# PEER layer tail on one core: four of the dense blocks' eight slots go to the ring of gathered V rows, and tile 0's products lead tile 1's by two blocks

## The chip, the core and the metric

The kernel runs on one core of a Trainium2 chip. The metric is the time of one execution on the device in microseconds (us), lower is better. The version before takes 1754.23 us, the median of 3 runs (1752.3 to 1754.84).

## What is computed

The reference is one decoder layer over 256 tokens of width 2048: attention and short convolution, an output projection, a layer norm, and then the channel mixing that this change is about. For each token it picks 8 heads x 16 experts out of 16384, and each expert is one row of 2048 floats in `expert_u` and one in `expert_v`:

```python
eid = i1 * N_KEYS + i2                      # N_KEYS = 128, 16384 experts
g = softmax(best_s)
a = gelu(einsum('td,thkd->thk', hx, expert_u[eid]))
y = einsum('thk,thkd->td', g * a, expert_v[eid])
out = layernorm(ALPHA * h + y)
```

All arrays are float32. A row is 8 KB, and one pick (one row for each of 128 tokens) is 1 MB. There are 256 picks: 2 tiles of 128 tokens, 8 heads (a head of a tile is a unit, n = 0 to 15), 16 picks k each. In the kernel a pick has the number m = 16 n + k.

## The kernel before, in words

The engines run their own programs and wait for one another on semaphores. The order of each engine's work is written out by hand.

**U.** GpSimd gathers the 256 picks of `expert_u` by indirect DMA into a ring of RU = 8 slots (`gather_u`). VectorE takes the dot product of each with the tokens (`dot`, L1764), which counts `dots_done` and frees the slot.

**V, picks 0 to 143.** GpSimd also gathers the picks of `expert_v`, into a ring of RV = 7 slots (`gather_v`, L542 for units 0 to 13, L545 for units 14 and 15). TensorE adds the first PE_PICKS = 144 of them into PSUM with diagonal weights (L976), which counts `v_used`.

**V, picks 144 to 255.** VectorE adds these to `xh` (`add_row`, L1799), in the order of m, once its dots are all done. Each addition is followed by a drain that counts `v_dve`, and the gather of pick m waits for the addition of pick m - 7. This stage begins at 1409.9 us of the trace. Ahead of pick 246 VectorE waits for tile 0's four PSUM banks (`t0_sum`, L1851), ahead of pick 248 it waits for the two rows of layer norm 2 and finishes tile 0 (L1811, L1856, L1859), ahead of pick 253 it adds tile 1's banks (`t1_sum`, L1863), and behind pick 255 comes tile 1's layer norm (L1867 to L1874) with its output.

**Dense blocks.** The last FD = 40 of the 128 first keys, 5120 rows of `expert_v`, are not gathered for units 0 to 13: the gather has a bound (`bounds_check=ROWS - 1`), and a pick at or above it brings no row. These rows are read whole instead, as 40 blocks of 128 rows (1 MB each), by SyncE's DMA (L429). TensorE multiplies each block with a matrix of coefficients of tile 0 and one of tile 1: `dense_mm(t, f)` at L946 is four matmuls of 128x512. The matrices themselves are made by `hot_rows` (VectorE), `dense_rows` (TensorE, L938) and `dense_out` (ScalarE). The blocks lie in the eight slots of the U ring, free once U has ended: block f goes to slot f % 8. The first eight wait for the last dots, the others for tile 1's product:

```python
for f in range(FD):
    if f < RD:
        sp.wait_ge(S["dots_done"], TOPK * NU - RU + f + 1)
    else:
        sp.wait_ge(S["dense_used"], f - RD + 1)
```

and TensorE's order is

```python
for f in range(FD + LEAD):
    if f < FD:
        pe.wait_ge(s_d[f % RD], 16 * (f // RD + 1))
        dense_mm(0, f)
    if f >= LEAD:
        dense_mm(1, f - LEAD)
```

with LEAD = 3: the products of tile 0 run three blocks ahead of those of tile 1, and a slot is free when tile 1's product of its block has ended (`dense_used`). Behind block 39 SyncE issues the loads of the two rows of layer norm 2 (L431).

Of the kernel before, what the change touches and what calls it, by code (L numbers as in the profile page):

```python
# [7 lines left out]
ALU = mybir.AluOpType  # L8
# [21 lines left out]
TOPK = 16  # L30
NU = 16
RU = 8
RV = 7
# [2 lines left out]
PH = 8  # L36
V0_PICKS = TOPK * PH
PE_PICKS = V0_PICKS + TOPK
RD = 8
FD = 40  # L40
FA = 24
ROWS = (NKEY - FD) * NKEY
LEAD = 3
G_TOK = 8
NG_T = P // G_TOK
PICKS = (P, P - 2 * TOPK)
# [1 line left out]
IDS_AT.update({(n, 1): n + 1 for n in range(1, 9)})  # L48
HOT0_AT = {180 + 5 * b // 2: b for b in range(NG_T)}
HOT1_AT = {14 * TOPK + 5 + 3 * b // 2: b for b in range(NG_T)}  # L50
HTW = SEQ + 2
TCOL = (slice(0, P), slice(P + 2, SEQ + 2))
JOBS = [(0, (0,)), (1, (0,)), (0, (1,)), (1, (1,))] + [(h, (0, 1)) for h in range(2, PH)]
# [69 lines left out]
def build(nc, x, w_in, cmp_k_pos, cmp_k_w1, cmp_k_b1, cmp_k_w2, cmp_v_pos, cmp_v_w1, cmp_v_b1, cmp_v_w2,  # L123
# [15 lines left out]
    def at(name, shape, dt, offset=None):  # L139
        n = 2 if dt is BF16 else 4  # L140
        for s in shape[1:]:
            n *= s
        if offset is None:
            offset, top[0] = top[0], top[0] + (n + 31) // 32 * 32
        assert offset + n <= nc.sbuf_usable_end, name
        return nc.alloc_sbuf_tensor_at(name, shape, dt, offset=offset)
# [14 lines left out]
    xh = at("xh", [P, 2, D], F32, oc + 16 * K)  # L161
# [59 lines left out]

    hT = at("hT", [P, KC, HTW], F32, o_act)
    mixr = at("mixr", [P, KC, P], F32, o_act + 16 * K + 512)
# [35 lines left out]
    gate = at("gate", [P, NU, TOPK], F32, o_lo + 5 * K)  # L259
# [7 lines left out]
    eps2 = at("eps2", [P, 1], F32, o_lo + 6 * K + 448)  # L267
    qp = at("qp", [P, 2, 2, HTW], F32, o_lo + 6 * K + 512)
    stT = at("stT", [2, 2, P], F32, o_lo + 11 * K)
# [10 lines left out]
    v_home = [oc + 64 * K + 8 * K * i for i in range(4)] + [oc + 32 * K, oc + 40 * K, o_act]  # L280
    u_slot = [at(f"u_slot{i}", [P, D], F32, u_home[i]) for i in range(RU)]
    v_slot = [at(f"v_slot{i}", [P, D], F32, v_home[i]) for i in range(RV)]
    diag = at("diag", [P, 2, TOPK, P], F32, oc + 48 * K)
    sum0 = at("sum0", [P, D], F32, oc + 56 * K)
    ln2g_sb = at("ln2g_sb", [P, D], F32, oc + 48 * K)
# [29 lines left out]
    S = {n: nc.alloc_semaphore(n) for n in names}  # L315
# [5 lines left out]
    s_wb = [nc.alloc_semaphore(f"s_wb{i}") for i in range(4)]  # L321
    s_u = [nc.alloc_semaphore(f"s_u{i}") for i in range(RU)]
    s_v = [nc.alloc_semaphore(f"s_v{i}") for i in range(RV)]
    s_d = [nc.alloc_semaphore(f"s_d{i}") for i in range(RD)]

    def bview(i, *shape):
# [37 lines left out]
    def _(sp):  # L364
# [58 lines left out]
# [5 lines that stand above are left out]
            first = ROWS + NKEY * f  # L428
            sp.dma_start(u_slot[f % RD][:, :], expert_v[0][first:first + NKEY, :]).then_inc(s_d[f % RD], 16)  # L429
        for row, src in ((ln2g_sb, ln2_g), (ln2b_sb, ln2_b)):  # L430
# [11 lines left out]
    def _(pool):  # L442
# [86 lines left out]
        def gather_v(n, k):  # L529

            m = TOPK * n + k
            if m == 0:
                pool.wait_ge(S["wq_used"], 12)
            if m == EARLY_V:
                pool.wait_ge(S["wq_used"], 16)
            if RV <= m < PE_PICKS + RV:
                pool.wait_ge(S["v_used"], m - RV + 1)
            if m >= PE_PICKS + RV:
                pool.wait_ge(S["v_dve"], m - RV - PE_PICKS + 1)
            src = bass.IndirectOffsetOnAxis(ap=eid[:, n, k:k + 1], axis=0)  # L540
            if n < NU - 2:
                nc.gpsimd.indirect_dma_start(out=v_slot[m % RV][:, :], out_offset=None, in_=expert_v[0], in_offset=src,  # L542
                                             bounds_check=ROWS - 1, oob_is_err=False).then_inc(s_v[m % RV], 16)
            else:
                nc.gpsimd.indirect_dma_start(out=v_slot[m % RV][:, :], out_offset=None, in_=expert_v[0], in_offset=src  # L545
                                             ).then_inc(s_v[m % RV], 16)

        for m in range(TOPK * AHEAD):
            gather_u(m // TOPK, m % TOPK)
            if m == TOPK * AHEAD - 9:  # L550
                for k in range(EARLY_V):
                    gather_v(0, k)
        sent = TOPK * AHEAD
        for m in range(EARLY_V, TOPK * NU):
            while sent < min(TOPK * NU, TOPK * AHEAD + (m + 1) * 13 // 10):
                gather_u(sent // TOPK, sent % TOPK)
                sent += 1
            if m == PE_PICKS:
                while sent < TOPK * NU:
                    gather_u(sent // TOPK, sent % TOPK)  # L560
                    sent += 1
            gather_v(m // TOPK, m % TOPK)
# [3 lines left out]
    def _(pe):  # L566
# [375 lines left out]
        def dense_mm(t, f):  # L942

            src = dense0[:, f, :] if t == 0 else dense1[f >= FA][:, f - FA * (f >= FA), :]
            for q in range(4):
                ins = nc.tensor.matmul(bank[(4 if t == 0 else 0) + q][:, :], src, u_slot[f % RD][:, 512 * q:512 * q + 512],  # L946
                                       start=False, stop=(f == FD - 1))
                if f == FD - 1:
                    ins.then_inc(S[("t0_sum", "t1_sum")[t]], 1)
            if t and f < FD - RD:  # L950
                ins.then_inc(S["dense_used"], 1)
# [30 lines left out]
        for q in range(4):  # L982
            nc.tensor.matmul(bank[4 + q][:, :], ident[:, :], sum0[:, 512 * q:512 * q + 512], start=True, stop=False)
# [7 lines that stand above are left out]
# [381 lines left out]
    def _(dve):  # L1372
        V = nc.vector
# [404 lines left out]
        def hot_rows(t, b):  # L1778

            g, n = NG_T * t + b, PICKS[t]  # L1780
            cols = slice(G_TOK * b, G_TOK * b + G_TOK)
            if b == 0:
                dve.wait_ge(S["pick_ok"], t + 1)
            if g >= 2:
                dve.wait_ge(S["dense_mm"], g - 1)
            row, key, coef = (pickT[0:n, t, i, cols].unsqueeze(2) for i in range(3))
            V.tensor_tensor(hot1[0:n, g % 2, :, :], iota_row[0:n, :].unsqueeze(1).to_broadcast([n, G_TOK, FD]),
                            row.to_broadcast([n, G_TOK, FD]), ALU.is_equal)
            V.tensor_tensor(hot2[0:n, g % 2, :, :], iota_key[0:n, :].unsqueeze(1).to_broadcast([n, G_TOK, NKEY]),
                            key.to_broadcast([n, G_TOK, NKEY]), ALU.is_equal)  # L1790
            dve.drain()
            V.tensor_tensor(hot1[0:n, g % 2, :, :], hot1[0:n, g % 2, :, :], coef.to_broadcast([n, G_TOK, FD]), ALU.mult
                            ).then_inc(S["hot_ok"], 1)

        def add_row(m):

            n, k = divmod(m, TOPK)
            dve.wait_ge(s_v[m % RV], 16 * (m // RV + 1))
            V.scalar_tensor_tensor(xh[:, 1, :], v_slot[m % RV][:, :], gate[:, n, k:k + 1], xh[:, 1, :], ALU.mult, ALU.add)  # L1799
            dve.drain().then_inc(S["v_dve"], 1)  # L1800

        def stats_of(t):
# [16 lines left out]
        for n in range(NU):  # L1819
            for k in range(TOPK):  # L1820
# [15 lines left out]
                m = TOPK * n + k  # L1836
                if m in HOT0_AT:
                    hot_rows(0, HOT0_AT[m])
                if m in HOT1_AT:
                    hot_rows(1, HOT1_AT[m])  # L1840
        for b in range(len(HOT1_AT), NG_T):
            hot_rows(1, b)
        V.tensor_scalar(xh[:, 1, :], xh[:, 1, :], ALPHA, None, ALU.mult)
        dve.drain()
        for m in range(PE_PICKS, TOPK * NU):
            if m == PE_PICKS + TOPK:
                gates_of(NU - 1)
            if m == TOPK * NU - 10:
                for q in range(4):
                    dve.wait_ge(S["t0_sum"], q + 1)  # L1850
                    V.bn_stats(l2st[:, 0, q, :], bank[4 + q][:, :])  # L1851
                stats_of(0)
            if m == TOPK * NU - 8:
                dve.wait_ge(S["s_ln2row"], 32)
                root_inverse(0)
                V.scalar_tensor_tensor(y0[:, :], psum_all[:, 4:8, :].rearrange("p a b -> p (a b)"), l2mv[:, 0, 0:1],  # L1856
                                       ln2g_sb[:, :], ALU.subtract, ALU.mult)
                dve.drain()
                V.scalar_tensor_tensor(y0[:, :], y0[:, :], l2rs[:, 0:1], ln2b_sb[:, :], ALU.mult, ALU.add  # L1859
                                       ).then_inc(S["final_ok"], 1)  # L1860
            if m == TOPK * NU - 3:
                dve.wait_ge(S["t1_sum"], 4)
                V.tensor_tensor(xh[:, 1, :], xh[:, 1, :], psum_all[:, 0:4, :].rearrange("p a b -> p (a b)"), ALU.add)  # L1863
                dve.drain()
            add_row(m)
# [35 lines left out]
```

## Time and profile before

| | before |
|---|---|
| median of 3 runs | 1754.23 us (1752.3 to 1754.84) |
| the profiled execution, its own time | 1752.67 us |
| its span, first to last instruction | 1750.9 us |
| mean granted TensorE clock | 0.933 |
| VectorE busy | 1360.2 us (78%) |
| TensorE matmul busy | 1487.4 us (85%) |
| DMA, mean over the span | 351 GB/s |
| dense loads, issue to landing (median of 40) | 8.8 us |

All times of the trace are counted from the span's start. The 1752.67 us of the profiled execution are its span and 1.8 us around it. TensorE's matmul time is written by the profiler's model of pipelined instructions; a group of a float32 product shows 8 matmul instructions for the four of the program. "Idle before" is the time in which an engine had nothing running ahead of an instruction, with the one whose end let it go. A DMA's time to landing runs from its issue to its semaphore. PEclk is the granted TensorE clock in parts of full speed (2.4 GHz; the other level is half of it).

### The profile page before, as it was taken

How to read it: one execution, taken by the hardware profiler on the slowest of the kernel's cores; microseconds unless marked ns; L12 is line 12 of the kernel's file. 1: busy time of each engine (PE TensorE's matmuls, PEld its weight loads, DVE VectorE, ACT ScalarE, POOL GpSimd, SP SyncE). 2: the span in 40 equal slices, each digit the busy share in tenths (PEclk: the TensorE clock that was granted, in tenths of full speed). 3: DMA queues.
4: the chain of work that ended last, by engine and by line, in shares of the span. 5: the costliest groups of instructions: out<-in, count | busy, mean ns of one | idle time of the engine just before them, and what ended most of it. 6: DMA issues, size and time to landing. Idle time of an engine off the chain costs nothing.

```text
span 1750.9 us, 16867 instructions
## 1 busy us (share of the span) xinstructions
PE 1487.4 (85%) x6164; PEld 931.8 (53%) x6164; DVE 1360.2 (78%) x1915; ACT 380.5 (22%) x822; POOL 967.4 (55%) x591
## 2 busy tenths in 40 slices
PE   8999999999979906887777877888989899999940
PEld 7988999988668702333333333344445644444420
DVE  6666656666897999767868788977876988788798
ACT  5665455564201212101010101020220100000000
POOL 3210000000364677887777767786785887688581
PEclk9999999999989957989998999999999899999975
DMA  9876443466799999999999999999999999999994
GB/s 319 279 262 217 121 145 121 145 203 230 297 380 412 374 424 425 412 425 426 421 424 426 415 425 422 420 426 409 415 427 360 377 414 409 401 404 410 423 428 186
DMA packets 159379, 615.38 MB, mean 351 GB/s; under 512 B 20915, under 2 KB 74255, under 8 KB 96703
## 3 DMA queue, kind: packets, MB, share of 16 engines
q0 software_dynamic: 79232, 485.32, 67.6%
q1 hardware_dynamic: 80064, 128.99, 20.7%
q8 instruction: 48, 0.79, 0.2%
q14 instruction: 35, 0.29, 0.0%
HBM read 683.42 MB, written 2.10 MB: 392 GB/s over the span
## 4 chain that ended last, share of the span: by engine, by line
PE 29%; POOL 19%; DMA 19%; DVE 18%; issue 12%; DVEq 2%; ACT 1%; SPq 0%; POOLq 0%; ACTq 0%
DMA v_slot<-in_expert_v_dram,eid 15%; PE psum_all L587 13%; POOL v_slot L542 11%; DVE u_slot L1764 9%; POOL u_slot L525 9%; PE psum_all L727 4%; DVE xh L1799 4%; PE psum_all L976 3%; DMA u_slot<-in_expert_u_dram,eid 2%; PE psum_all L752 2%; PE psum_all L708 1%; PE psum_all L614 1%; PE psum_all L612 1%; PE psum_all L938 1%; DMA wq_ring<-in_w_query_dram 0%
## 5 line engine op out<-in xcount | busy, mean ns | idle before, releaser
L976 PE MATMUL psum_all<-v_slot,diag 128*128 128x512 f32 x1152 | 557.2, 636 | 154.5 <-DMA v_slot<-in_expert_v_dram,eid 108.9
L1764 DVE SCALAR_TENSOR_TENSOR u_slot<-u_slot,xh 128x2048 f32<-128x2048 f32 x256 | 576.2, 2287 | 91.3 <-DMA u_slot<-in_expert_u_dram,eid 90.0
L525 POOL DMA_INDIRECT u_slot<-in_expert_u_dram,eid x256 | 441.7, 1726 | 302.7 <-DVE u_slot L1764 136.7
L542 POOL DMA_INDIRECT v_slot<-in_expert_v_dram,eid x224 | 424.6, 1895 | 94.5 <-issue 64.7
L976 PEld LDWEIGHTS psum_all<-v_slot,diag 128*128 128x128 f32 x1152 | 224.1, 202 | 464.1 <-issue 255.4
L1799 DVE SCALAR_TENSOR_TENSOR xh<-v_slot,gate,xh 128x2048 f32<-128x2048 f32 x112 | 263.4, 2352 | 53.9 <-DMA v_slot<-in_expert_v_dram,eid 46.3
L1382 DVE TENSOR_TENSOR w_lo<-w_ring,w_hi 128x512 fp32r<-128x512 f32 x240 | 156.6, 688 | 78.3 <-ACT w_hi L1012 75.1
L587 PE MATMUL psum_all<-act_hi,w_hi 128*128 128x256 f32 x640 | 185.2, 289 | 1.1 <-DVE w_lo L1382 1.0
L587 PE MATMUL psum_all<-act_hi,w_lo 128*128 128x256 f32 x640 | 181.1, 283 | 0.0
L587 PE MATMUL psum_all<-act_lo,w_hi 128*128 128x256 f32 x640 | 181.0, 283 | 0.0
L1012 ACT ACTIVATE w_hi<-w_ring 128x512 fp32r<-128x512 f32 x240 | 139.4, 622 | 42.7 <-PE psum_all L587 41.5
L946 PE MATMUL psum_all<-u_slot,dense 128*128 128x512 f32 x320 | 143.4, 592 | 0.0
L752 PE MATMUL psum_all<-hT,wq_ring 128*128 128x258 f32 (+2 forms) x640 | 119.6, 346 | 11.9 <-DMA wq_ring<-in_w_query_dram 11.9
L587 PEld LDWEIGHTS psum_all<-act_hi,w_hi 128*128 128x128 f32 x640 | 122.4, 191 | 13.3 <-issue 4.1
L587 PEld LDWEIGHTS psum_all<-act_lo,w_hi 128*128 128x128 f32 x640 | 122.5, 191 | 2.8 <-issue 0.5
L587 PEld LDWEIGHTS psum_all<-act_hi,w_lo 128*128 128x128 f32 x640 | 122.5, 191 | 0.0
L752 PEld LDWEIGHTS psum_all<-hT,wq_ring 128*128 128x128 f32 x640 | 104.4, 194 | 27.9 <-DMA wq_ring<-in_w_query_dram 12.3
L513 POOL DMA_DIRECT2D skeys<-in_sub_keys_dram x1 | 1.2, 1165 | 198.1 <-PE psum_all L587 198.1
L946 PEld LDWEIGHTS psum_all<-u_slot,dense 128*128 128x128 f32 x320 | 60.8, 190 | 76.5 <-issue 76.5
L946 PE MATMUL psum_all<-u_slot,dense1a 128*128 128x512 f32 x192 | 86.3, 592 | 0.0
L545 POOL DMA_INDIRECT v_slot<-in_expert_v_dram,eid x32 | 64.2, 2005 | 34.2 <-DVEq L1800 26.6
L938 PEld LDWEIGHTS psum_all<-hot,hot 128*128 128x128 f32 (+1 forms) x512 | 65.2, 200 | 19.3 <-issue 13.6
(283 smaller groups left out, 1484.2 us busy)
## 6 DMA issues: line engine op xcount, KB each, us to landing
w_ring<-in_w_in_dram SPq DMA_DIRECT2D x88, 512.0 KB, 4.9
u_slot<-in_expert_v_dram SPq DMA_DIRECT2D x40, 1024.0 KB, 8.8
wo_ring<-in_w_out_dram SPq DMA_DIRECT2D x32, 512.0 KB, 5.0
wq_ring<-in_w_query_dram SPq DMA_DIRECT2D x32, 512.0 KB, 8.9
w_ring<-in_cmp_k_w_dram POOLq DMA_DIRECT2D x16, 512.0 KB, 5.7
w_ring<-in_cmp_v_w_dram POOLq DMA_DIRECT2D x16, 512.0 KB, 4.4
u_slot<-in_expert_u_dram,eid POOLq DMA_INDIRECT x256, 19.2
v_slot<-in_expert_v_dram,eid POOLq DMA_INDIRECT x256, 18.2
```

The lines of the kernel that those rows point to most:

```text
L525: nc.gpsimd.indirect_dma_start(out=u_slot[m % RU][:, :], out_offset=None, in_=expert_u[0], in_offset=bass.IndirectOffsetOnAxis(ap=eid[:, n ...
L542: nc.gpsimd.indirect_dma_start(out=v_slot[m % RV][:, :], out_offset=None, in_=expert_v[0], in_offset=src, bounds_check=ROWS - 1, oob_is_er ...
L587: ins = nc.tensor.matmul(o, st, mv, start=(k == 0 and b == 0 and i == 0), stop=(k == KC - 1 and i == 2), skip_group_check=True)
L727: ins = nc.tensor.matmul(bank[acc + b][:, :], st[:, k, half], mv[:, n % RING, :], start=(i == 0 and m == 0), stop=(i == KC - 1 and m == 2))
L752: ins = nc.tensor.matmul(bank[QBANK[h % 2] + c][:, cols], wq_ring[j % 2][:, k // 4, k % 4, 256 * (h % 2) + 128 * c:256 * (h % 2) + 128 * c ...
L938: ins = nc.tensor.matmul(bank[4 * t + g % 2][:, FD * i:FD * i + FD], hot2[0:n, g % 2, i, :], hot1[0:n, g % 2, i, :], start=True, stop=True ...
L946: ins = nc.tensor.matmul(bank[(4 if t == 0 else 0) + q][:, :], src, u_slot[f % RD][:, 512 * q:512 * q + 512], start=False, stop=(f == FD - 1))
L976: ins = nc.tensor.matmul(bank[(4 if n < PH else 0) + q][:, :], diag[:, n % 2, k, :], v_slot[m % RV][:, 512 * q:512 * q + 512], start=(m in ...
L1012: nc.scalar.activation(w_hi[:, n % RING, :], raw_item(n), ACT.Copy).then_inc(S["hi_done"], 1)
L1382: V.tensor_tensor(w_lo[:, n % RING, :], raw_item(n), w_hi[:, n % RING, :].bitcast(F32), ALU.subtract).then_inc(S["lo_done"], 1)
L1764: V.scalar_tensor_tensor(u_slot[m % RU][:, :], u_slot[m % RU][:, :], 1.0, xh[:, n // PH, :], ALU.mult, ALU.mult, accum_out=u_dot[:, n, k:k ...
L1799: V.scalar_tensor_tensor(xh[:, 1, :], v_slot[m % RV][:, :], gate[:, n, k:k + 1], xh[:, 1, :], ALU.mult, ALU.add)
```

## The change

`RD`, the number of slots for dense blocks, goes from 8 to 4: block f goes to U slot f % 4, and its load waits for tile 1's product of block f - 4. `LEAD` goes from 3 to 2. U slots 4 to 7 are appended to the V ring as its places 7 to 10. Picks up to 150 keep their places (m % 7). From m = 151 (`LATE`) on, the ring has 11 places, taken in the order of `RING_V`: first U slots 4 to 7, for picks 151 to 154, which wait for the dots 253 to 256; then the seven old places, whose gathers wait for the addition of pick m - 11. `v_place(m)` gives the place, `v_times(m)` how often it has been filled.

```diff
-RD = 8
+RD = 4
-LEAD = 3
+LEAD = 2
+LATE = V0_PICKS + TOPK + RV
+RING_V = list(range(RV, RV + RU - RD)) + [m % RV for m in range(V0_PICKS + TOPK, LATE)]
...
+def v_place(m):
+    return m % RV if m < LATE else RING_V[(m - LATE) % len(RING_V)]
+
+
+def v_times(m):
+    return sum(1 for i in range(m + 1) if v_place(i) == v_place(m))
...
     v_slot = [at(f"v_slot{i}", [P, D], F32, v_home[i]) for i in range(RV)]
+    v_slot += u_slot[RD:]
...
     s_v = [nc.alloc_semaphore(f"s_v{i}") for i in range(RV)]
+    s_v += [nc.alloc_semaphore(f"s_e{i}") for i in range(RU - RD)]
     s_d = [nc.alloc_semaphore(f"s_d{i}") for i in range(RD)]
...
-            if m >= PE_PICKS + RV:
-                pool.wait_ge(S["v_dve"], m - RV - PE_PICKS + 1)
+            if LATE <= m < LATE + RU - RD:
+                pool.wait_ge(S["dots_done"], TOPK * NU - RU + v_place(m) - RV + RD + 1)
+            if m >= LATE + RU - RD:
+                pool.wait_ge(S["v_dve"], m - len(RING_V) - PE_PICKS + 1)
```

The rest of the diff puts `v_place(m)` and `v_times(m)` where `m % RV` and `m // RV + 1` stood, in `gather_v` and in `add_row`.

## Rows read from the trace of the kernel before

**Rows 1.** The page: DMA busy in tenths, 40 slices

```profile
DMA  9876443466799999999999999999999999999994
```

**Rows 2.** Windows: PE, PEld, DVE, ACT, POOL busy (x), PEclk, DMA share, GB/s

```profile
1475.00:1500.00 25.00, 25.00 (x60) 11.08 (x59) 18.56 (x9) 0.00 (x0) 19.74 (x9) 1.00 1.00 402
1675.00:1700.00 25.00, 9.47 (x23) 3.86 (x21) 23.80 (x11) 0.00 (x0) 21.95 (x11) 0.76 1.01 428
```

**Rows 3.** Waits by engine from 1409 us on: total, times, longest

```profile
DVE xh L1799 <- DMA v_slot<-in_expert_v_dram,eid: 46.3, 49, 2.6
```

**Rows 4.** Timeline of VectorE: start, us, instructions, idle before them

```profile
1409.93 7.30 DVE L1799 SCALAR_TENSOR_TENSOR xh<-v_slot,gate,xh 128x2048 f32<-128x2048 f32 x3
1418.35 2.35 DVE L1799 SCALAR_TENSOR_TENSOR xh<-v_slot,gate,xh 128x2048 f32<-128x2048 f32 x1 [1.11 <-DMA v_slot<-in_expert_v_dram,eid]
...
1658.88 44.35 DVE L1799 SCALAR_TENSOR_TENSOR xh<-v_slot,gate,xh 128x2048 f32<-128x2048 f32 x18 [1.96 <-DMA v_slot<-in_expert_v_dram,eid]
1703.35 2.49 DVE L1851 BATCH_NORM_STATS2 l2st<-psum_all 128x6 f32<-128x512 f32 x4
...
1711.80 2.35 DVE L1856 SCALAR_TENSOR_TENSOR y<-psum_all,l2mv,ln2g_sb 128x2048 f32<-128x2048 f32 x1
...
1728.84 2.29 DVE L1863 TENSOR_TENSOR xh<-xh,psum_all 128x2048 f32<-128x2048 f32 x1
```

**Rows 5.** Timeline of TensorE: dense products, early and at the end

```profile
1423.37 3.60 PE L946 MATMUL psum_all<-u_slot,dense1a 128*128 128x512 f32 x8
1426.81 3.60 PE L946 MATMUL psum_all<-u_slot,dense 128*128 128x512 f32 x8
...
1667.14 3.60 PE L946 MATMUL psum_all<-u_slot,dense 128*128 128x512 f32 x8
1670.57 13.90 PE L946 MATMUL psum_all<-u_slot,dense1b 128*128 128x512 f32 x32
```

**Rows 6.** Timeline of SyncE: one dense load, and the last loads

```profile
1427.00 0.33 SPq L429 DMA_DIRECT2D u_slot<-in_expert_v_dram  x1
...
1639.87 0.33 SPq L429 DMA_DIRECT2D u_slot<-in_expert_v_dram  x1
```

**Rows 7.** Dense loads to landing: issued 1425-1622, 1622-1650, 1380-1400

```profile
DMA to landing us min/median/max: 8.2/8.7/9.5
DMA to landing us min/median/max: 9.0/9.4/9.5
DMA to landing us min/median/max: 10.0/11.1/12.2
```

**Rows 8.** Timeline of TensorE: a product that waited, and the next

```profile
1318.03 3.70 PE L976 MATMUL psum_all<-v_slot,diag 128*128 128x512 f32 x8 [0.89 <-DMA v_slot<-in_expert_v_dram,eid]
1321.57 1.88 PE L938 MATMUL psum_all<-hot,hot 96*128 96x40 f32 x16
```

**Rows 9.** Landing: gathers 1475-1500, 1600-1625; dense loads in these windows

```profile
DMA to landing us min/median/max: 17.3/19.0/19.8
DMA to landing us min/median/max: 12.8/13.9/15.2
DMA to landing us min/median/max: 8.4/8.6/8.8
DMA to landing us min/median/max: 8.3/8.4/8.6
```

**Rows 10.** Timeline of GpSimd: gathers 149 and 151

```profile
1400.47 10.25 POOL L542 DMA_INDIRECT v_slot<-in_expert_v_dram,eid  x1 [0.30 <-issue]
...
1413.46 2.17 POOL L542 DMA_INDIRECT v_slot<-in_expert_v_dram,eid  x1 [0.30 <-issue]
```

**Rows 11.** DMA issues: size, median us to landing

```profile
ln2b_sb<-in_ln_b_dram SPq DMA_DIRECT2D x1, 1024.0 KB, 17.9
```

**Rows 12.** Windows ahead of the dense stage, as rows 2

```profile
1200.00:1225.00 25.00, 23.06 (x86) 12.85 (x85) 16.62 (x18) 1.31 (x3) 15.60 (x10) 0.93 0.98 399
1225.00:1250.00 25.00, 23.74 (x86) 12.52 (x84) 22.68 (x24) 8.82 (x23) 18.60 (x11) 1.00 1.00 408
```

More of the change, by code:

```diff
@@ L537, in gather_v @@
                 pool.wait_ge(S["v_used"], m - RV + 1)
-            if m >= PE_PICKS + RV:
-                pool.wait_ge(S["v_dve"], m - RV - PE_PICKS + 1)
+            if LATE <= m < LATE + RU - RD:
+                pool.wait_ge(S["dots_done"], TOPK * NU - RU + v_place(m) - RV + RD + 1)
+            if m >= LATE + RU - RD:
+                pool.wait_ge(S["v_dve"], m - len(RING_V) - PE_PICKS + 1)
             src = bass.IndirectOffsetOnAxis(ap=eid[:, n, k:k + 1], axis=0)
             if n < NU - 2:
-                nc.gpsimd.indirect_dma_start(out=v_slot[m % RV][:, :], out_offset=None, in_=expert_v[0], in_offset=src,
-                                             bounds_check=ROWS - 1, oob_is_err=False).then_inc(s_v[m % RV], 16)
-            else:
-                nc.gpsimd.indirect_dma_start(out=v_slot[m % RV][:, :], out_offset=None, in_=expert_v[0], in_offset=src
-                                             ).then_inc(s_v[m % RV], 16)
+                nc.gpsimd.indirect_dma_start(out=v_slot[v_place(m)][:, :], out_offset=None, in_=expert_v[0], in_offset=src,
+                                             bounds_check=ROWS - 1, oob_is_err=False).then_inc(s_v[v_place(m)], 16)
+            else:
+                nc.gpsimd.indirect_dma_start(out=v_slot[v_place(m)][:, :], out_offset=None, in_=expert_v[0], in_offset=src
+                                             ).then_inc(s_v[v_place(m)], 16)
         for m in range(TOPK * AHEAD):
@@ L1797, in add_row @@
             n, k = divmod(m, TOPK)
-            dve.wait_ge(s_v[m % RV], 16 * (m // RV + 1))
-            V.scalar_tensor_tensor(xh[:, 1, :], v_slot[m % RV][:, :], gate[:, n, k:k + 1], xh[:, 1, :], ALU.mult, ALU.add)
+            dve.wait_ge(s_v[v_place(m)], 16 * v_times(m))
+            V.scalar_tensor_tensor(xh[:, 1, :], v_slot[v_place(m)][:, :], gate[:, n, k:k + 1], xh[:, 1, :], ALU.mult, ALU.add)
             dve.drain().then_inc(S["v_dve"], 1)
```

## The prediction

> **What bounds the kernel now.** I read the page first [rows 1]. No compute engine fills the span, but the 16 DMA engines stand at nine tenths or more from the twelfth slice to the last but one. So the tail, where the change works, is first of all a matter of who gets the DMA. The windows of 25 us [rows 2] say how the tail looks inside: in the dense stage TensorE is never idle (25.00 of 25 us) and the DMA share is 1.00 at 402 GB/s, while VectorE has gaps (18.56 us busy); once the dense blocks are in, the DMA moves 428 GB/s and VectorE has 23.80 us of its own work. The waits [rows 3] give these gaps a sum: 46.3 us in 49 waits for gathered V rows. VectorE's timeline [rows 4] gives them a place: they lie between 1418 and 1659 us. Once the dense loads are over (the last is issued at 1639.87 [rows 6]) the eighteen additions from 1658.88 run without a gap, 2.47 us each (44.35 for 18, with the drains between), and so does all that follows to the end. The end of the kernel is therefore VectorE's: from the first statistics of tile 0 at 1703.35 to the end of the span at 1750.9 there are 47.5 us of its work and of the output, with no wait worth a line.
>
> TensorE has no say in that end. Its timeline [rows 5] has one dense product of four matmuls every 3.433 us (1423.37 to 1426.81), a pair of them, tile 0's and tile 1's, every 6.87 us. Tile 0's last product starts at 1667.14 and ends at 1670.7, and the statistics that need it start at 1703.35: 32.6 us of slack. Tile 1's last product ends at 1684.5 and is needed at 1728.84 [rows 4]. The question is what the change does with this slack.
>
> **Part 1, the dense loads with four slots and a lead of two.** I call iteration j the pair that starts with tile 0's product of block j and goes on with tile 1's of block j - 2. The slot of block j - 4 is free at the end of iteration j - 2. Load j is issued then, and iteration j, the next but one, needs it. Between lies one iteration, 6.87 us. (Before, with eight slots and a lead of three, a slot was free at the end of iteration j - 5 and the load had four iterations, 27.5 us. That is why no wait is seen.)
>
> How long does a load take from slot to product? Three terms. From tile 1's product to the issue: the first such load goes at 1427.00 [rows 6], the next product starts at 1426.81 [rows 5], so 0.2 us. From issue to landing: 8.7 us in the median of 29 loads from 1425 to 1622, 8.2 at least, 9.5 at most, and 9.4 for the three behind 1622, when the gathers bring whole picks (units 14 and 15 have no bound) [rows 7]. From landing to the restarted product: a product that waited for its gather holds TensorE for 3.54 us until the next instruction in place of 3.43 (1318.03 to 1321.57 [rows 8]), 0.11 us, and I add 0.04 for the wake-up. Sum 0.2 + 8.7 + 0.15 = 9.05 us, against 6.87 that are covered. TensorE waits 2.18 us.
>
> Not at every block, though. If iteration j waits, iteration j + 1 does not: its load left at the end of iteration j - 1, and when iteration j starts late by 2.18, the next starts 6.87 later still, 2.18 + 6.87 = 9.05 behind that load's start. The recurrence is start(j) = the larger of start(j-1) + 6.87 and start(j-2) + 6.87 + 9.05, and it gives one wait in every two blocks: at 4, 6, ... 38, 18 waits. The gathers without a bound start at pick 224; in the changed kernel they are issued from about 1590 us on (80 additions from 1409.93 at 2.5 to 2.6 us, less the 11 of the ring), so I take the last 6 waits at 9.4 + 0.35 - 6.87 = 2.88 and the first 12 at 2.18. Sum 12 x 2.18 + 6 x 2.88 = 26.2 + 17.3 = 43.4 us.
>
> The smaller lead also moves tile 0's last product behind one more of tile 1's: without waits it would start at 1670.57 and end at 1674.2 [rows 5]. With them it ends at 1674.2 + 43.4 = 1717.6. The last of the four statistics (0.62 us each [rows 4]) ends 0.6 us later, at 1718.2. Before it ended at 1703.35 + 2.49 = 1705.8. **Difference +12.4 us.** Behind it follow the same additions and norms as before, 45.1 us to the end of the span. Tile 1's last product comes 10.3 us behind tile 0's (three more products) and is needed 23 us behind the statistics: hidden.
>
> Bounds: with every load at the shortest of the tail, 8.2, a wait is 1.68 and the sum 30.2, so tile 0's sum ends at 1704.4 and the statistics at 1705.0: -0.8 us. With every load at 9.5, 18 x 2.98 = 53.6: +22.6 us. The loads issued from 1380 to 1400 took 10.0 to 12.2 [rows 7], but they followed each other more closely than one load's time and lay behind one another in their queue; here the spacing is 6.87 or 9.05 us. At 10.0 the same sum gives +31.6, at 11.1 +51.4.
>
> Does the longer V ring slow the loads? The gathers' own times say how much stands in their queue: 19.0 us to landing from 1475 to 1500, 13.9 from 1600 to 1625. The dense loads of the same windows took 8.6 and 8.4 [rows 9]. So a queue of gathers that is a third deeper moves a dense load by 0.2 us, and I keep 8.7. The Trainium skill, "DMA: Bandwidth & Descriptors", section "Queues, rings and completion order", has it the same way: an engine takes turns between the queues it has work for, packet by packet, so the depth of the other queue would not matter. The section "Anatomy of one DMA" of the same page of the Trainium skill has some 2.0 us fixed and 436 GB/s (fitted to GpSimd's DMAs); with half the turns for a load of 1 MB, that is an estimate of 2.0 + 2 x 2.4 = 6.8 us, a wait of 0.3 us in place of 2.18, and no loss at all. The measured 8.7 us speaks against it, and the sum goes by the measurement.
>
> **Part 2, eleven places for V.** The gathers stay on GpSimd's one queue. Gather 149 stands from 1400.47 to 1410.7, 150 is next, and 151 starts at 1413.46 [rows 10]. All dots are over when the additions begin at 1409.93 [rows 4]. So the new, earlier permission of pick 151 (dot 253) brings nothing: the queue in front of it is what holds it. From 153 on the gathers no longer wait for an addition seven picks back. The bytes do not change (112 gathers, 40 blocks), nor does the DMA share of 1.00, so what VectorE wins of its 46.3 us is what the dense loads give up: with 43 us of waits the dense stream is about five blocks behind at 1650, which is five to seven picks for V, or some 12 us. VectorE would then reach pick 246 at about 1691 (in no case before 1703.35 - 46.3 = 1657) and stand there until tile 0's sum is done. The gain is real and is thrown away ahead of t0_sum. I cost it at zero; its cover is the wait for TensorE.
>
> **Part 3, what else moves.** Dense loads 4 to 7, issued behind the last dots before, now leave from 1423 on [rows 5]. That helps the first V rows (VectorE waits less around 1420), and again ends in the same wait: zero. The two rows of layer norm 2 stand behind load 39 on SyncE. Load 39 now leaves at about 1704 in place of 1639.87 [rows 6], the second row at 1705.3. At 17.9 us [rows 11] it lands at 1723, and its use, ahead of tile 0's norm, comes at 1711.7 + 12.4 = 1724 [rows 4]. It just fits, and the gathers are nearly over by then, so I take zero; without that relief it could cost one or two us. SyncE has nothing else queued before the outputs.
>
> **The sum.** Profiled execution 1752.67 + 12.4 = 1765.1 us. It lay 1.6 below the median of the runs, so in terms of the median 1754.23 + 12.4 = 1766.6; I say 1766.
>
> **The rivals.**
>
> *Same: the loads come in at their shortest.* With 8.2 us throughout, the working above gives -0.8 us, 1753.5. For it: dense traffic is thinner (one block in 7.96 us in place of 6.87), and where the gathers' queue was shorter the loads were a little shorter too [rows 9]. Against: V takes up what dense leaves, and the whole picks at the end cost 9.4.
>
> *Faster: a lone load lands in under 8 us, and the V ring's gain comes through.* The place is the same wait for t0_sum. If x is the wait per two blocks, tile 0's sum ends at 1674.2 + 18x, and VectorE arrives at about 1703.4 - 5.4x (12 us for 2.2). They meet at x = 1.25, that is at a load of 7.8 us and 1696.7 us: about 6.7 us saved, 1747.5. It decides for faster from about 8.0 us down. For it: the 46.3 us are there to be won [rows 3]. Against: of 29 loads none was under 8.2. The Trainium skill's figures ("DMA: Bandwidth & Descriptors", the estimate of 6.8 us above) would end near here, with VectorE as the later one and 1 to 3 us saved.
>
> *Slower by more: the clock.* In the dense stage TensorE now has no idle time and its clock is at full speed [rows 2]. With 2 us of idle time in every 16 it may lose it at times. In the stage ahead, one window with 1.9 us of idle time has 0.93 and the next 1.00 [rows 12]; 0.93 of 25 us is 3.5 us at half speed, 1.75 us lost. Over 300 us, twelve windows, at every second one: some 10 us of delay at most, part of it inside waits. 3 to 9 us on top, 1769 to 1775.
>
> *Slower by much: loads of 10 us and more under eleven gathers.* +31.6 to +51.4, 1786 to 1805. For it: the one row with such values. Against: what was said of it above.
>
> **How the numbers follow.** A difference under 0.2% (3.5 us) can't be told from none here. Chances: the forecast, +8 to +18 us (1762 to 1772), 0.60; the clock on top 0.12; much longer loads 0.12; same 0.08; faster 0.08. Slower is then 0.84, same 0.08, faster 0.08. The range takes in the forecast, the clock, the case of no difference and the low end of the long loads: 1753 to 1786. That leaves out faster and the upper half of the long loads, some 0.15.
>
> **What the profile after would show.** TensorE's dense stage has about 18 waits of some 2 us for the dense loads, at every second block, and ends near 1728 in place of 1684. Load to landing stays at 8.4 to 9.4. VectorE's waits for V rows fall from 46.3 to some 25 us, and a new one of 15 to 25 us stands ahead of L1851, put down to TensorE. The stretch from L1851 to the end is unchanged. The prediction is wrong if the loads land much faster or slower than 8.7 us, if the waits come at every block, or if VectorE reaches pick 246 behind TensorE, which would make the V rows the bound.

## The result and the profile after

The changed kernel takes 1769.46 us (median of 6 runs, 1763.38 to 1773.33); the kernel before, timed beside it, 1753.39. The ratio is 1.0093, 95% interval 1.0071 to 1.0115: slower by 16 us. The profiled execution took 1773.25 us, the second slowest of the six, with a span of 1771.5: 20.6 us more than the span before.

Waits of the changed kernel from 1409 us on (total, times, longest):

```profile
PE psum_all L962 <- DMA u_slot<-in_expert_v_dram: 34.9, 25, 2.9
DVE l2st L1867 <- PE psum_all L962: 33.9, 4, 33.4
DVE xh L1815 <- DMA v_slot<-in_expert_v_dram,eid: 21.1, 17, 2.6
...
DVE xh L1815 <- DMA u_slot<-in_expert_v_dram,eid: 12.0, 13, 1.9
```

Before there was one line of this weight [rows 3]. Now TensorE waits for dense loads, which it never did, and VectorE stands 33.4 us in one piece ahead of tile 0's statistics. Its waits for V rows (now under two names, since four places are U slots) have come down from 46.3 to 33.1 us.

TensorE's timeline of the dense stage, to be held against [rows 5]. First the start of the stage in the kernel before:

```profile
1409.64 13.90 PE L946 MATMUL psum_all<-u_slot,dense 128*128 128x512 f32 x32
```

Then the stage of the changed kernel:

```profile
1407.67 10.46 PE L962 MATMUL psum_all<-u_slot,dense 128*128 128x512 f32 x24
...
1469.87 3.70 PE L962 MATMUL psum_all<-u_slot,dense 128*128 128x512 f32 x8 [1.52 <-DMA u_slot<-in_expert_v_dram]
...
1478.26 3.70 PE L962 MATMUL psum_all<-u_slot,dense 128*128 128x512 f32 x8 [1.26 <-DMA u_slot<-in_expert_v_dram]
...
1659.86 3.70 PE L962 MATMUL psum_all<-u_slot,dense 128*128 128x512 f32 x8 [2.31 <-DMA u_slot<-in_expert_v_dram]
...
1666.83 3.60 PE L962 MATMUL psum_all<-u_slot,dense 128*128 128x512 f32 x8
...
1676.78 6.78 PE L962 MATMUL psum_all<-u_slot,dense 128*128 128x512 f32 x8 [2.92 <-DMA u_slot<-in_expert_v_dram]
...
1722.06 3.60 PE L962 MATMUL psum_all<-u_slot,dense 128*128 128x512 f32 x8
1725.49 10.46 PE L962 MATMUL psum_all<-u_slot,dense1b 128*128 128x512 f32 x24
```

The lines show three things. Up to block 17 (1533) there is a wait of about 1 us at every block. From then on there is one of 1.4 to 2.9 us at every second block, as at 1659.86 and 1676.78 with none at 1666.83. And six products are longer than 3.70 us (5.20 to 6.78), each of them behind a wait: for part of their time the clock was at the lower of its two levels. Of the twelve windows of 25 us from 1425 to 1725, the five that hold such a product have a PEclk of 0.80 or 0.93, the seven others one of 1.00.

The loads themselves took what they took before (8.8 us there), by the page's DMA issues (size, median us to landing):

```profile
u_slot<-in_expert_v_dram SPq DMA_DIRECT2D x40, 1024.0 KB, 8.7
```

VectorE's timeline, against [rows 4]:

```profile
1682.43 7.29 DVE L1815 SCALAR_TENSOR_TENSOR xh<-v_slot,gate,xh 128x2048 f32<-128x2048 f32 x3 [2.60 <-DMA v_slot<-in_expert_v_dram,eid]
1723.12 0.70 DVE L1867 BATCH_NORM_STATS2 l2st<-psum_all 128x6 f32<-128x512 f32 x1 [33.40 <-PE psum_all L962]
...
1725.69 0.70 DVE L1867 BATCH_NORM_STATS2 l2st<-psum_all 128x6 f32<-128x512 f32 x1 [0.16 <-PE psum_all L962]
```

Pick 246 is reached at 1723.12 - 33.40 = 1689.7 in place of 1703.35, 13.6 us earlier, and all of it is lost. (2.3 us of the 13.6 are no gain of the change: in this execution the additions began at 1407.60, in that of the kernel before at 1409.93. In the other executions they began at 1407.2 to 1409.6.) From the end of the fourth statistic to the end of the span there are 1771.5 - 1726.4 = 45.1 us, as before.

The chain of waits that ends last now runs through the dense loads (start, us, what):

```profile
by line: DMA u_slot<-in_expert_v_dram 44.6%; PE psum_all L962 41.9%; DVE xh L1815 6.2%; DVE xh L1890 0.9%; issue 0.8%; DVEq L1816 0.7%; DVE y L1875 0.7%; DVE y L1872 0.7%; DVE xh L1879 0.7%; DVEq L1889 0.6%; DVE l2st L1883 0.6%; DVE xh L188
...
1687.02 8.76 DMA u_slot<-in_expert_v_dram
1695.82 8.85 PE psum_all L962 x16
1704.68 8.66 DMA u_slot<-in_expert_v_dram
1713.39 12.28 PE psum_all L962 x24
```

It is a ring of two links: a load of 8.7 us, the products that free the next slot, the next load. Before, no dense load was in the chain from 1410 us on: it was made of gathers of V rows (44.6% of it their DMA, 16.8% GpSimd's part) and of VectorE's additions (21.4%).

### The profile page after: what moved, and what is told of

It is laid out like the page before. It is cut to its first block, busy times and chain, and to the rows that moved or that the text cites. A ratio compares the mean times of both kernels' runs of the same rounds, so it can differ in the third digit from the quotient of the medians.

```text
span 1771.5 us, 16867 instructions
## 1 busy us (share of the span) xinstructions
PE 1507.8 (85%) x6164; PEld 935.2 (53%) x6164; DVE 1360.2 (77%) x1915; ACT 380.5 (21%) x822; POOL 961.3 (54%) x591
## 4 chain that ended last, share of the span: by engine, by line
PE 37%; DMA 18%; DVE 17%; POOL 15%; issue 9%; DVEq 2%; ACT 1%; SPq 0%; POOLq 0%; ACTq 0%
PE psum_all L603 13%; DVE u_slot L1780 10%; DMA u_slot<-in_expert_v_dram 9%; PE psum_all L962 9%; POOL u_slot L539 8%; POOL v_slot L558 7%; DMA v_slot<-in_expert_v_dram,eid 5%; PE psum_all L743 4%; DMA u_slot<-in_expert_u_dram,eid 4%; PE psum_all L992 2%; PE psum_all L768 1%; DVE xh L1815 1%; PE psum_all L724 1%; PE psum_all L954 1%; PE psum_all L630 1%
## 5 line engine op out<-in xcount | busy, mean ns | idle before, releaser
L539 POOL DMA_INDIRECT u_slot<-in_expert_u_dram,eid x256 | 451.6, 1764 | 296.0 <-DVE u_slot L1780 130.0
L558 POOL DMA_INDIRECT v_slot<-in_expert_v_dram,eid x196 | 352.2, 1797 | 61.1 <-issue 58.2
L1815 DVE SCALAR_TENSOR_TENSOR xh<-v_slot,gate,xh 128x2048 f32<-128x2048 f32 x72 | 169.3, 2351 | 27.6 <-DMA v_slot<-in_expert_v_dram,eid 21.1
L962 PE MATMUL psum_all<-u_slot,dense 128*128 128x512 f32 x320 | 157.8, 640 | 34.9 <-DMA u_slot<-in_expert_v_dram 34.9
L1815 DVE SCALAR_TENSOR_TENSOR xh<-u_slot,gate,xh 128x2048 f32<-128x2048 f32 x40 | 94.1, 2353 | 15.2 <-DMA u_slot<-in_expert_v_dram,eid 12.0
```

What stands on the lines that cost most here:

```text
L539: nc.gpsimd.indirect_dma_start(out=u_slot[m % RU][:, :], out_offset=None, in_=expert_u[0], in_offset=bass.IndirectOffsetOnAxis(ap=eid[:, n ...
L558: nc.gpsimd.indirect_dma_start(out=v_slot[v_place(m)][:, :], out_offset=None, in_=expert_v[0], in_offset=src, bounds_check=ROWS - 1, oob_i ...
L1815: V.scalar_tensor_tensor(xh[:, 1, :], v_slot[v_place(m)][:, :], gate[:, n, k:k + 1], xh[:, 1, :], ALU.mult, ALU.add)
```

## The experiments

Ratios are to the kernel before, timed on the same chip in the same measurement.

**Without the V part.** The V ring keeps seven places, four dense slots and the lead of two stay.

```diff
-RING_V = list(range(RV, RV + RU - RD)) + [m % RV for m in range(V0_PICKS + TOPK, LATE)]
+EXTRA = 0
+RING_V = list(range(RV, RV + EXTRA)) + [m % RV for m in range(V0_PICKS + TOPK, LATE)]
...
-            if LATE <= m < LATE + RU - RD:
+            if LATE <= m < LATE + EXTRA:
...
-            if m >= LATE + RU - RD:
+            if m >= LATE + EXTRA:
```

> The change without its V part: four dense slots and a lead of two, but the V ring keeps its seven places; U slots 4 to 7 lie unused. Theory A (a dense load is covered by one iteration of 6.87 us and takes 9 us, the V ring has no say): TensorE waits for dense loads as in the changed kernel (about 35 us of idle time in some 25 waits), VectorE's waits for V rows are 35 to 46 us, tile 0's sum still comes last, time 1763 to 1773 us. Theory B (eleven queued gathers slow the dense loads): with seven, loads land in 8 us or less, few waits, 1750 to 1756 us.

1767.21 us, ratio 1.0095 (1.0071 to 1.0118), the same as the whole change, with 30 waits of TensorE that sum to 33.4 us. Loads land in 8.8 us in the median, with seven places for gathers as with eleven. Theory B falls: the longer V ring does not slow the loads. What the ring does is seen in the wait ahead of the statistics:

```profile
1715.71 0.70 DVE L1868 BATCH_NORM_STATS2 l2st<-psum_all 128x6 f32<-128x512 f32 x1 [17.03 <-PE psum_all L963]
```

VectorE arrives at 1698.7; with eleven places it came at 1689.7 (the additions began at 1407.35 and 1407.60). The ring is worth 9 us of arrival when the dense loads run late, and nothing of the end.

**A lead of one.** `LEAD = 1` in the changed kernel.

> The changed kernel with a lead of one in place of two: a slot is free one iteration earlier, so a load is covered by two iterations (13.7 us). Theory A: no waits for dense loads, tile 0's sum ends at about 1678 us, full clock through the stage, VectorE comes last at its additions; time 1747 to 1754 us, that is none or a small gain over the kernel before, since the DMA is full either way. Theory C (four slots are too few whatever the lead): waits stay, 1763 us or more.

1753.94 us, ratio 1.0010 (1.0002 to 1.0019). All waits for dense loads are gone, with the same four slots, and the loads still take 8.7 us. Theory C falls. But the V ring of eleven brings nothing: VectorE waits 31.8 + 16.1 = 47.9 us for V rows, against 46.3 with seven places [rows 3], and reaches pick 246 at 1705.6. V rows come sooner only if the dense loads take less of the DMA.

**Five slots, a lead of three.** `RD = 5`, `LEAD = 3`, a V ring of ten.

> Five dense slots with the old lead of three, a V ring of ten. One slot more than in the changed kernel, but again one iteration of cover (slots less lead less one). Theory A: waits as in the changed kernel, 25 or so with 35 us of idle time, 1763 to 1773 us. Theory C (the number of slots counts): 1750 to 1760 us.

1766.79 us, ratio 1.0084 (1.0069 to 1.0098), 22 waits of TensorE with 37.4 us. That is one slot more than in the kernel with a lead of one, and the time is 13 us longer. What counts is slots less lead less one, the number of iterations that cover a load.

**The lead of two alone.** `LEAD = 2` in the kernel before.

> The kernel before with the smaller lead alone (two in place of three, eight dense slots, V ring of seven). Theory A: no waits, tile 0's sum ends at about 1674, 29 us before it is needed: no difference, within 0.1%. Rival (the smaller lead itself costs): 1755 us or more.

1752.63 us, ratio 0.9995 (0.9986 to 1.0004), no waits, VectorE's waits 47.0 us. With eight slots the smaller lead costs nothing.

**A filler against the clock.** The changed kernel with one more matmul per iteration; the weights are zeros, written by VectorE into a buffer that is no longer used.

```diff
             if f >= LEAD:
                 dense_mm(1, f - LEAD)
+                if f == LEAD:
+                    pe.wait_ge(S["zero_ok"], 1)
+                if f < FD - 1:
+                    nc.tensor.matmul(bank[0][:, :], hot2[:, 0, 0, :], hot2[:, 1, 0:4, :].rearrange("p a b -> p (a b)"), start=False, stop=False)
```

> The changed kernel with one more matmul of 128x512 behind each of tile 1's products but the last (zero weights, so it adds nothing to the sum), about 0.86 us each, 37 or so. It fills TensorE's waits. Theory A with the clock (the loads set the pace at about 8 us for a block; on top of it TensorE lost 11 us in six slow products because it had idle time): waits below 0.5 us each, all products at 3.6 us, tile 0's sum some 42 us late and no more, time 1761 to 1766 us, and runs closer together than the 10 us of the changed kernel. Rival (the slow products are not a matter of idle time): slow products remain and the time is 1769 us or more.

1766.51 us (1765.69 to 1769.32), ratio 1.0086 (1.0072 to 1.0100). No product is longer than 3.70 us. Waits are left, more than expected: twelve, 8.2 us in sum, the longest 1.3. Windows of the changed kernel and of this one (columns as in [rows 2]):

```profile
1675.00:1700.00 25.00, 21.25 (x38) 8.97 (x39) 11.16 (x5) 0.00 (x0) 6.81 (x4) 0.80 1.01 426
```

```profile
1675.00:1700.00 25.00, 24.31 (x56) 10.20 (x55) 9.76 (x5) 0.00 (x0) 5.82 (x4) 1.00 1.01 427
```

PEclk is 0.80 against 1.00, with the same load time (8.7 us). Tile 0's last product starts at 1714.71 in place of 1722.06, 7.3 us earlier, against the 11.4 us of the six slow products; the difference is a stage that began 0.4 us later and 3.7 us more of waits and fillers. The runs lie within 3.6 us of one another with the filler, and within 10 without it. But the intervals of the two ratios overlap: the medians stand 15.0 us above the kernel before with the filler and 16.1 without it. So it is shown that the filler removes the slow products; that it shortens the median of this kernel is not. For another kernel the next pair shows it.

**Eight slots, a lead of six, without and with the filler.** From the kernel before, with `LEAD = 6` only, and then with the same filler. Again one iteration of cover, but the V ring of seven and the first eight blocks of the kernel before.

> The kernel before with a lead of six: eight dense slots and a V ring of seven as before, but a load is again covered by one iteration only (8 - 6 - 1). Tile 0's last product is three products earlier (1660.5 without waits). Theory A: from block 8 on about 16 waits of 2.2 us (35 us), and some 5 to 10 us of slow clock, so tile 0's sum ends at 1700 to 1706; meanwhile the V rows get the DMA that the dense loads give up and VectorE reaches pick 246 at about 1697 in place of 1703.35. Time 1746 to 1753 us. Theory C (eight slots are enough): no waits at all, 1751.6 us.

1756.73 us (1751.19 to 1760.36), ratio 1.0018 (1.0005 to 1.0031). There are 18 waits with 32.8 us: TensorE stands as long with eight slots as with four when the lead eats them. The time suffers less, because with the longer lead four products fewer stand ahead of tile 0's last one (13.7 us). It lies above the 1746 to 1753 us that were expected: six slow products again cost 11.4 us, and tile 0's last product ended at 1708.8, not by 1706. VectorE reached pick 246 at 1691.9, tile 0's first bank came at 1706.3.

> The same with the filler matmul (zero weights, adds nothing) behind tile 1's products. Theory A: the clock stays full, tile 0's sum ends at about 1697, VectorE arrives at the same time, time 1744 to 1750 us, the best so far. Rival (VectorE's arrival is set by the DMA alone and does not move): 1751 us or more.

1750.24 us (1747.22 to 1753.85), ratio 0.9986 (0.9976 to 0.9996): 0.14% below the kernel before. The interval ends 0.0004 short of one, and this is the lowest of twelve variants, so a gain over the kernel before is likely and not shown. The gain over the same kernel without the filler is shown: the two intervals do not touch, and the difference is 0.3%, 5 to 6 us. No product is slow any more, and tile 0's last one starts at 1695.58 in place of 1705.20. Both engines now arrive together, and VectorE's wait for the banks is gone:

```profile
1697.78 2.49 DVE L1874 BATCH_NORM_STATS2 l2st<-psum_all 128x6 f32<-128x512 f32 x4
```

That is 5.6 us ahead of [rows 4], but 2.3 of it are additions that began at 1407.63 in place of 1409.93, and behind the statistics a new wait of 2.0 us for a V row appears (at 1705.11). From the start of the additions to the end of the span this execution is 1.6 us shorter than that of the kernel before. VectorE's waits for V rows were 46.3 us before, 35.4 without the filler and 43.0 with it: slowing the dense loads a little gives V the DMA, and TensorE's slack pays for it.

**Seven slots, a lead of five, the filler, a V ring of eight.**

> Seven dense slots, a lead of five (again one iteration of cover), a V ring of eight, and the filler matmul (zero weights, adds nothing). Against eight slots and a lead of six with the filler (0.14% below the kernel before) the V ring has one place more, and tile 0's sum comes one product later, at about 1700. Theory A: tile 0's sum then decides, 1750 to 1753 us. Rival (the V ring's place is worth more than that): below 1749 us.

1752.98 us, ratio 1.0001 (0.9991 to 1.0011). VectorE arrives at 1690.3 and waits 13.3 us for TensorE, so TensorE decides, as theory A had it. Tile 0's last product starts at 1702.36, 6.8 us later than in the kernel above and not the 3.4 of one product; it waited 1.25 us for its load, and where the rest comes from was not looked into. One place more for V brings nothing as long as TensorE comes last.

**The first eight blocks in eight slots.** With the lead of one: blocks 0 to 7 use all U slots, later ones slots 0 to 3; slots 4 to 7 join the V ring at pick 174.

```diff
-LATE = V0_PICKS + TOPK + RV
+LATE = 174
...
+def d_place(f):
+    return f if f < RU else f % RD
...
             if LATE <= m < LATE + RU - RD:
-                pool.wait_ge(S["dots_done"], TOPK * NU - RU + v_place(m) - RV + RD + 1)
+                pool.wait_ge(S["dense_used"], v_place(m) - RV + RD + 1)
```

> Lead of one, four dense slots and a V ring of eleven as in the kernel with a lead of one, but the first eight dense blocks still go to all eight U slots, loaded at the last dots; slots 4 to 7 join the V ring at pick 174 when their blocks are done. Theory D (four dense loads fewer at the last dots leave the DMA short of work from 1400 to 1425, 344 to 357 GB/s in place of 425, which costs some 4 us of DMA time): the window is back at 420 GB/s or more and the time is 1.5 to 4 us below that of the kernel with a lead of one, 1748 to 1751 us. Rival (the shortfall is made up later and costs nothing): the same time as with a lead of one, 0.1% above before.

1753.61 us, ratio 1.0005 (0.9996 to 1.0014). The window from 1400 to 1425 is back at 425 GB/s (357 with the lead of one, 344 in the changed kernel), but the ratio is only 0.05% below that of the kernel with a lead of one, inside both intervals. The missing loads cost 1 us or so, if anything; theory D's 1.5 to 4 us lie mostly above that, though the intervals do not exclude the lower end. VectorE's waits for V rows are 35.4 + 12.1 = 47.5 us here, so it was not the shortage of loads that kept the eleven places from helping.

**What the 8.7 us of a load are made of.** Three kernels split each load from block 4 on into two halves. In the first SyncE brings rows 0 to 63 and ScalarE, on a queue of its own, rows 64 to 127:

```diff
+            act.wait_ge(S["dense_used"], f - RD + 1)
+            act.dma_start(u_slot[f % RD][64:P, :], expert_v[0][first:first + 64, :]).then_inc(s_d[f % RD], 16)
```

> The changed kernel with each dense load from block 4 on split into two halves of 64 rows, one issued by SyncE as before and one by ScalarE, on a DMA queue of its own. Theory E (the 8.7 us of a load are its share against the gathers, about half of the DMA, so a third queue gives it two thirds): both halves landed after some 7.5 us, waits of 1 us in place of 2.2, TensorE's idle time for dense loads 5 to 15 us in place of 35, time 1752 to 1760 us. Theory F (the 8.7 us are mostly fixed, or the gathers hold their share): 8.5 us and more, time as in the changed kernel, 1765 to 1770 us.

> The control: the same two halves, both issued by SyncE on its one queue. Theory E: no gain, the second half lands after 8.7 to 9.3 us, time 1765 to 1771 us. If the two halves gain here too, it is the smaller size that helps and not the queue.

1845.02 us (ratio 1.0539, 1.0518 to 1.0559) on two queues and 1896.01 us (1.0826, 1.0801 to 1.0850) on one. No theory had this. The halves landed after 10.8 and 11.8 us (medians, 1450 to 1650) on two queues, 10.3 and 13.7 on one, and the gathers after 36.9 and 43.8 in place of 23.6 in the changed kernel. The DMA is as busy as ever and moves a quarter to a third less. The window from 1500 to 1525 with one queue:

```profile
1500.00:1525.00 25.00, 18.85 (x39) 7.93 (x38) 12.69 (x6) 0.00 (x0) 6.76 (x6) 0.86 1.02 280
```

Against 423 GB/s in the changed kernel. So I split by columns, each half to all 128 partitions:

```diff
-                sp.dma_start(u_slot[f % RD][0:64, :], expert_v[0][first:first + 64, :]).then_inc(s_d[f % RD], 16)
+                sp.dma_start(u_slot[f % RD][:, 0:1024], expert_v[0][first:first + NKEY, 0:1024]).then_inc(s_d[f % RD], 16)
...
-            act.dma_start(u_slot[f % RD][64:P, :], expert_v[0][first:first + 64, :]).then_inc(s_d[f % RD], 16)
+            act.dma_start(u_slot[f % RD][:, 1024:2048], expert_v[0][first:first + NKEY, 1024:2048]).then_inc(s_d[f % RD], 16)
```

> The changed kernel with each dense load from block 4 on split by columns: SyncE brings columns 0 to 1023 of all 128 rows, ScalarE columns 1024 to 2047, on two queues. Unlike halves of 64 rows, each half goes to all 128 partitions. Theory G (the halves of 64 rows cost 1845 and 1896 us because they use half of the partitions, not because of their number or size): the DMA stays above 400 GB/s, no such loss. Then theory E (share): the slower half lands after 7 to 8 us, TensorE's idle time for dense loads is 5 to 20 us in place of 35, time 1752 to 1762 us. Theory F (fixed cost, or the gathers keep their share): 8.5 us and more, 1764 to 1771 us. If theory G is wrong: 300 GB/s and 1840 us again.

1775.13 us (1767.29 to 1782.54), ratio 1.0118 (1.0098 to 1.0138). Theory G holds: the same window has 422 GB/s. Theory E falls: the halves landed after 8.1 and 9.0 us, so a load split over two queues is no sooner complete than a whole one in one queue. The time lies 4 us above what theory F had given. The queues' packets, MB and share of the DMA, 1450 to 1650, first in this kernel, then in the changed one:

```profile
q1 hardware_dynamic: 3344, 12.19, 15.4%
q10 hardware_dynamic: 3341, 12.18, 15.0%
```

```profile
q1 hardware_dynamic: 3522, 25.58, 30.7%
```

The dense loads have the same share on two queues (15.4% + 15.0%) as on one. Both halves were under way at the same time, so this run cannot tell a fixed time from a share that the gathers hold against two queues as against one. What the 8.7 us consist of stays open.

## Why the prediction was right

It gave 1766 us, range 1753 to 1786, slower at 0.84; measured were 1769.46. The mechanism was the one that the runs show; two of its details were not, and that the number came out so close is in part luck, as the account at the end of the second point shows.

- *The cover of a load.* Right. One iteration of cover, without the filler, gives 18 to 30 waits and 33 to 37 us of idle time with four slots, with five and with eight; two iterations or more give none, with four and with eight. Load to landing was 8.7 us in the median of the changed kernel, as taken. The 9.4 us taken for the last loads did not come: those issued from 1620 on had a median of 8.7 too.
- *The sum of the waits, 43.4 us.* Tile 0's last product ends 1722.06 + 3.60 - 1407.67 = 318.0 us after the stage began. Ahead of it lie 76 products, so without waits that would be 76 x 3.433 + 3.60 = 264.5 [rows 5]. 53.5 us were lost. The six slow products lasted 11.4 us more than 3.70 each; 42.1 us remain for the waits. The trace's own sum of idle time, 34.9 us in 25 waits, fits this: it counts from the end of a product, 0.17 us behind the point where the next would have started, and each restart holds TensorE for 0.11 us more (0.28 x 25 = 7). The term was good to 1.3 us.

  For the profiled execution the account is then 12.4 - 1.3 + 11.4 - 2.0 = 20.5 us, the 2.0 because its dense stage began at 1407.67 in place of 1409.64; measured were 20.6. So the forecast of 12.4 missed this execution by 8 us, and an earlier start hid 2 more. The slow products are not the same in every execution: the profiled one of the kernel with seven V places had three, 5.0 us in sum, and took 1765.81 us. That this is why the median lies nearer to the forecast is likely, but no run shows it.
- *"One wait in every two blocks."* Wrong, and it is one of the signs that the prediction itself named as showing it wrong ("if the waits come at every block"). For blocks 4 to 17 the same sum came as a wait at each block (1429.21 to 1533.23 for 13 of them, 8.0 us apart; the forecast's 15.92 for two is 7.96), and at every second one only after the first slow product. The step that failed is "if iteration j waits, iteration j + 1 does not": it holds only if the first wait takes the whole 2.18 us. The first late load landed in 7.6 us, its wait was 0.78, and the next block waited for the rest. The recurrence ties only start(j) to start(j-2), so both splits have the same sum, and the sign was badly chosen: waits at every block do not contradict the cover of one iteration.
- *The clock.* Put at nothing in the sum and held as a rival on top, 3 to 9 us at 0.12. It was there in the profile with 11.4 us, and the filler removed the slow products. How much of it is in the 3.7 us by which the median lies above the forecast (16.1 against 12.4) is not shown: with the filler and no slow product the same kernel still stands 15.0 us above the kernel before. In the pair with a lead of six the filler was worth 5 to 6 us. It should have been a term of the sum: idle time of some 2 us in every 16 came with slow products in all five kernels that had it without a filler (11.4, 5.0, 8.4, 11.4 and, with the loads split by columns, 12.7 us).
- *The V ring, zero.* Right in the end and in its mechanism: VectorE came at 1689.7 (forecast 1691) and stood 33.4 us (forecast 15 to 25, short by the clock, whose 11.4 us it had left out). Its waits for V rows fell to 33.1, not to 25; the 25 did not fit the forecast's own gain of 12 us, 46.3 - 12 = 34 does. I tied the gain to what the dense loads give up; the kernel with a lead of one shows that with the dense loads on time eleven places bring nothing.
- *Gather 151 is held by the queue.* Right: it left 2.4 us behind 150, as before. The rows of layer norm 2 were no wait. The shortage of the DMA from 1400 to 1425, 344 GB/s in place of 425, was not foreseen; where it was tried it costs about 1 us, which is within the noise.
- *The rival that ends faster* needed loads under 8 us, and their median was 8.7. Its other half, that TensorE's slack of 32 us can be traded for VectorE's waits, is what the kernel with eight slots, a lead of six and the filler does: 1750.24 us.

The estimate of 6.8 us from the Trainium skill ("DMA: Bandwidth & Descriptors", "Anatomy of one DMA" with the turns between queues) does not hold here: 8.6 to 8.8 us were measured in the median in every kernel with whole loads (those issued from 1418 us on). That the depth of the other queue does not matter, as the prediction took it from the same page's "Queues, rings and completion order", the runs bear out (8.8 us with seven places for gathers, 8.7 with eleven). Theory E, that a load on two queues would have two turns in three, they do not.

## What to carry to other kernels

A ring with S slots whose last reader runs L iterations behind its first covers a load by S - L - 1 iterations; count that, not the slots, and compare it with the load's time from issue to landing in the trace. Where the DMA is full, more buffers for one stream bring nothing unless another stream takes less: slack on one engine can be spent so, but only down to the point where the two arrive together. And a stage that is made to wait some 2 us at every second step can lose clock as well; a matmul with zero weights in each step can be cheaper than the idle time, as in the pair with a lead of six.

## What was not expected of the hardware

Loads of 64 partitions in place of 128, mixed with the gathers, brought the DMA from 423 to 280 GB/s at an unchanged busy share of 1.0 (window 1500 to 1525), and 323 when the halves lay on two queues; loads of 4 KB rows over 128 partitions kept it at 422. The two kernels with two queues have halves of the same size and number, so it is neither of these. They also differ in the length of a row, but whole loads have 8 KB rows like the slow halves, over 128 partitions, and keep 423. What is left is the number of partitions of a load; why it matters was not tried.

Each slow product of TensorE lasted 1.5 to 3.1 us longer, and all six in the changed kernel came directly behind a wait for a load of 1.9 to 2.9 us. Not every such wait had one: that of 2.31 us at 1659.86 had none, nor had one of 2.97 us with the loads split by columns. The waits of 0.4 to 1.5 us at each block, from 1429 to 1537, had none among them. What decides between them is not shown.
